# Probability-times-value products of a fused attention block: two 64-column tiles of TensorE for four 32-column ones

## The reference

```
def forgetting_attention(q, k, v, log_f):          # per block of 128 queries
    logits = einsum('bhqd,bhsd->bhqs', qq, k) * scale + cq[..., :, None] - c[:, :, None, :]
    p = masked_softmax(logits, kpos[None, :] <= tpos[:, None])
    return einsum('bhqs,bhsd->bhqd', p, v)         # the product that the change touches
# nsa_attention ends likewise: o_s = einsum(p_s, vg) and o_w = einsum(p_w, vw),
# both causal over the 512 keys here (8 blocks of 64, top 16; a window of 512)
```

## Time and profile before

| | us |
|---|---|
| median of three runs | 2138.06 |
| the profiled execution, its own time | 2140.45 |
| its span | 2138.6 |
| PE busy | 2098.0 (98%) |
| PE weight loads (PEld) busy | 1812.3 (85%) |
| POOL / DVE / ACT busy | 910.2 / 862.4 / 716.6 |
| share of L2359 in the chain that ended last | 2% |

### The profile page before, as it was taken

One profiled execution on the slowest core, in us unless ns is written; L12 is line 12 of the kernel. 1 busy time (PEld: TensorE's weight loads), 2 busy tenths in 40 slices (PEclk: granted clock), 3 DMA queues, 4 the chain that ended last, 5 costly groups with the idle time before them and its releaser, 6 DMA issues.

```text
span 2138.6 us, 38068 instructions
## 1 busy us (share of the span) xinstructions
PE 2098.0 (98%) x15700; PEld 1812.3 (85%) x15700; DVE 862.4 (40%) x1254; ACT 716.6 (34%) x1078; POOL 910.2 (43%) x690
## 2 busy tenths in 40 slices
PE   8999999999999999999999999999999899999998
PEld 7888888878777788887888999999999798998887
DVE  4222200676766432222107527832221545546302
ACT  5222221534678432223215432331222332222213
POOL 4444344435331444444444534434433044455442
PEclk9999999999999999999999999999999899999999
DMA  5323222431100232332222231122232022322221
GB/s 179 96 80 98 98 99 95 131 101 61 40 3 3 69 99 80 97 97 98 99 89 88 80 98 62 62 79 94 83 98 80 21 74 84 98 80 96 99 98 59
DMA packets 152200, 178.99 MB, mean 84 GB/s; under 512 B 6949, under 2 KB 142606, under 8 KB 152094
## 3 DMA queue, kind: packets, MB, share of 16 engines
q1 hardware_dynamic: 151931, 177.40, 25.6%
q10 hardware_dynamic: 163, 0.04, 0.0%
HBM read 175.34 MB, written 2.10 MB: 83 GB/s over the span
## 4 chain that ended last, share of the span: by engine, by line
PE 72%; issue 13%; POOL 8%; DVE 5%; ACT 1%; DMA 1%; SPq 0%; POOLq 0%; DVEq 0%; ACTq 0%
PE ps L1934 47%; PE ps L2075 11%; POOL wlo L681 8%; PE ps L2561 2%; PE ps L2359 2%; PE ps L2329 1%; PE ps L2342 1%; DVE tmp L1309 1%; PE ps L2201 1%; PE ps L2324 1%; PE ps L2171 1%; DMA raw<-in_ffn_wu 1%; PE ps L2368 0%; PE ps L2584 0%; PE ps L2574 0%
## 5 line engine op out<-in xcount | busy, mean ns | idle before, releaser
L681 POOL TENSOR_TENSOR wlo<-raw,whi 128x512 fp32r<-128x512 f32 x634 | 850.0, 1373 | 1092.1 <-ACT whi L770 1087.8
L1934 PE MATMUL ps<-xh,whi 128*128 128x258 f32 (+2 forms) x2400 | 687.5, 333 | 1.0 <-POOL wlo L681 0.7
L1934 PE MATMUL ps<-xh,wlo 128*128 128x258 f32 (+2 forms) x2400 | 682.4, 331 | 0.0
L1934 PE MATMUL ps<-xl,whi 128*128 128x258 f32 (+2 forms) x2400 | 680.5, 330 | 0.0
L770 ACT ACTIVATE whi<-raw 128x2048 fp32r<-128x2048 f32 (+1 forms) x158 | 301.3, 1907 | 787.1 <-PE ps L1934 484.4
L1934 PEld LDWEIGHTS ps<-xh,whi 128*128 128x128 f32 x2400 | 407.1, 189 | 52.1 <-issue 2.5
L1934 PEld LDWEIGHTS ps<-xh,wlo 128*128 128x128 f32 x2400 | 406.2, 189 | 45.5 <-issue 1.9
L1934 PEld LDWEIGHTS ps<-xl,whi 128*128 128x128 f32 x2400 | 405.8, 189 | 43.6
L2075 PE MATMUL ps<-act_h,wlo 128*128 (+1 forms) x528 | 208.6, 395 | 0.0
L2075 PE MATMUL ps<-act_l,whi 128*128 (+1 forms) x528 | 208.6, 395 | 0.0
L2075 PE MATMUL ps<-act_h,whi 128*128 (+1 forms) x528 | 208.6, 395 | 0.0
(11 more groups left out here) (348 smaller groups left out, 2380.1 us busy)
## 6 DMA issues: line engine op xcount, KB each, us to landing
raw<-in_w_in SPq DMA_DIRECT2D x47, 1024.0 KB, 5.1
raw<-in_ffn_wg SPq DMA_DIRECT2D x22, 1024.0 KB, 5.4
raw<-in_ffn_wu SPq DMA_DIRECT2D x22, 1024.0 KB, 5.4
raw<-in_ffn_wd SPq DMA_DIRECT2D x22, 1024.0 KB, 4.8
raw<-in_w_up SPq DMA_DIRECT2D x22, 1024.0 KB, 5.1
raw<-in_w_down SPq DMA_DIRECT2D x11, 1024.0 KB, 4.9
raw<-in_w_out SPq DMA_DIRECT2D x8, 1024.0 KB, 5.0
raw<-in_ple_w_gate SPq DMA_DIRECT2D x4, 1024.0 KB, 5.0
```

Source lines behind the costliest of these rows:

```text
L681: last = nc.gpsimd.tensor_tensor(wlo[:, slot, d], raw[:, slot, d], whi[:, slot, d].bitcast(F32), ALU.subtract)
L1934: last = mm(ps[:, j * banks + b, 0:n], w[:, k, e * P:(e + 1) * P], x[:, k, c0:c0 + n], start=(k == 0 and q == 0), stop=(k == KD - 1 and q ...
```

## The change

The loop over c takes steps of HD = 64 in place of 32. Each key block is now two products with 64 stationary columns, where it was four with 32. Operands, moving columns, PSUM banks, accumulation over k, and every wait and signal stay as they are.

```diff
                         for k in range(i + 1):
-                            for c in range(0, P, 32):
-                                last = mm(ps[c:c + 32, 6 + q % 2, 0:HD], probT[:, q % 3, k, c:c + 32], vtok[:, k, v0:v0 + HD],
+                            for c in range(0, P, HD):
+                                last = mm(ps[c:c + HD, 6 + q % 2, 0:HD], probT[:, q % 3, k, c:c + HD], vtok[:, k, v0:v0 + HD],
                                           start=(k == 0), stop=(k == i))
                     last.then_inc(pv_done, 1)
```

## The result

| | before | changed kernel |
|---|---|---|
| median of 10 runs each, us | 2138.01 (2134.95 to 2140.64) | 2146.05 (2140.12 to 2148.89) |
| ratio, with its 95% interval | | 1.003 (1.002 to 1.004) |
| the profiled execution: time, span | 2140.45, 2138.6 | 2143.18, 2141.3 |

The changed kernel is slower by 0.3%, about 6 us by the ratio; the two medians lie 8 us apart. Timed twice more beside the kernel before, it gave 1.0017 (1.0007 to 1.0026) and 1.0030 (1.0017 to 1.0043). All three intervals lie above 1. I had forecast 2140.0 us and no change that can be measured. The measured median lies at the very top of my range (0.05 us above it).

The account below looks back on a forecast made before the run. TensorE was taken to bound the attention loop, with about 1% idle. Wide products were to add 0.7 to 3.0 us, middle 1.9, all seen: 2138.06 + 1.9 = 2140.0 us (+0.09%), range 2135 to 2146.

Parts of the forecast that it names:

- 3.0 us for the attention: Upper end of the 0.7 to 3.0 us that L2359's wide products were to add over 96 steps.
- the clock behind it: Rival: after the attention, the half-clock stretch over L2368 falls otherwise, -2.35 to +2.35 us; chance 0.14, 0.07 above +0.2%.
- some 2 for the scatter: Range's allowance of some 2 us for the spread of runs (4.2 us apart) and later low-clock stretches.
- the 0.11 that I gave to a slower kernel: Chance of over 0.2% slower: 0.04 for wide tiles in series plus 0.07 for the clock.
- wide tiles in series: Rival: in L2359, accumulating wide tiles don't run side by side; +0.11 us a key block, +26 us, 2164; chance 0.04.
- What bounds the attention: Attention loop: TensorE bounds it, busy 34.56 of 35 us, with only about 4.6 us of true waits.
- the turn from a full-array transpose to part-array products: Before L2359's weight loads: claimed source of 0.17 us idle each, 15.0 of 19.6 us over 88 idle times.
- The pace of the wide tiles: L2359: a key block takes 0.115 to 0.120 us for 0.11, priced from L2480 and L2218.
- the number of instructions as a price of TensorE's array: Rival: 0.0036 us saved for each of 960 instructions in L2359, -3.5 us, 2134.6; chance 0.06.
- 4 ns for each further tile: Skill page's rule applied to L2359: two tiles for four save 16 ns a key block, 3.8 us in all.
- How much lies on the path: Attention: all 1.9 us counted as seen; 1.3 if a third were hidden in the 4.6 us of waits.
- Nothing is moved past anything, no wait or DMA is added, and no queue sees another order.: Claim on the whole change, which takes away 960 loads and 960 MATMULs and widens the other 960 of each.

Follow-up runs that it names:

- e4: Kernel before, with one full-array product in place of four tiles where a step has one key block; 2147.8 us, ratio 1.0040.
- e12: Kernel before with 48 tiny products (192 instructions) added at the start; 2151.5 us, ratio 1.0068.
- e2: Changed kernel with 32 tiny products (128 instructions) added at the start, putting its stream back; 2142.1 us, ratio 1.0012.
- e10: The same kernel as e2, timed again: changed kernel plus 128 instructions at the start; 2141.8 us, ratio 1.0021.

## Why the prediction was right or wrong

**The number: luck.** The range's top of 2146 was made of 3.0 us for the attention, 2.35 for the clock behind it and some 2 for the scatter. The attention took 1.4 and the clock behind it gave some back. That the median still came out at the top of the range is not to the credit of these terms. The forecast of 2140.0 us was 6 us low, and the 0.11 that I gave to a slower kernel stood on the clock and on wide tiles in series; it was neither.

**What bounds the attention: right.** TensorE, with its few true waits. But the 0.17 us before L2359's loads are not "the turn from a full-array transpose to part-array products": e4 has them before a full-array product. What sets them stays open. The forecast doesn't hang on it, since they stayed at 0.17.

**The pace of the wide tiles: right.** Four key blocks were to take 0.60 to 0.62 us to the next load and take 0.61; three were to take 0.48 to 0.50 and take 0.50. Wide tiles do run side by side while they accumulate; that rival is out, and so is the one on the number of instructions as a price of TensorE's array: no gain is to be seen. By the Trainium skill's rule of 4 ns for each further tile ("TensorE: Matmul & The Clock Gate", "Measured speedup vs the span model") the attention would have been 3.8 us shorter, an estimate from that page; it got longer.

**How much lies on the path: a little off.** I counted all 1.9 us; 1.4 are seen. The products themselves, from a step's first load to the next line's load, take 31, 25, 21 and 16 ns more with four, three, two and one key blocks (medians of the two traces), 2.2 us in all, so about a third was hidden. The waits for the other engines shrank where they stood: those in front of L2359's loads, which the earlier trace rows have at 9.0 and 10.6 us, are now

```profile
PEld ps L2359 <- issue: 11.4, 58, 0.6
PEld ps L2359 <- ACT probT L1074: 7.5, 30, 1.0
```

They are 88 idle times as before and 0.7 us shorter in sum; those down to ScalarE's copy fell from 9.0 to 7.5 us. They took up that part of the longer products. The 1.4 us lie within my 0.7 to 3.0. They hold over the other traces too: where the low-clock stretch at the loop's start is 6.8 us long the first to last L2359 take 132.7 to 132.9 us with 32-column tiles and 134.2 to 134.3 with 64-column ones.

**The step that failed** is this sentence on the change: "Nothing is moved past anything, no wait or DMA is added, and no queue sees another order." It is true of the order and missed the place. 1920 instructions fewer move all that follows in TensorE's stream by half a block, and 600 us later the bursts wait for their blocks four times and not once: 4.5 us more of breaks in the profiled executions, and 3.9 us more for the stage, since waits for VectorE got shorter. With the attention's 1.4 this makes 5.3; the mean difference over all executions is 5.0 +- 0.6 us. The two profiled executions themselves lie only 2.7 us apart, because the changed one has less low clock late in the second block: from 1656 to 1700 us the clock before is 0.77, from 1660 to 1700 after it is 0.83, and the part behind the stage is 2.4 us shorter. The single pair of traces gives the mechanism, the many executions the size. The breaks also answer for the sign of my error. I had priced fewer instructions as nothing or as a gain, and the on which I did so all lie where the stream keeps up. The kernel before had a hint that I left unread: its own 1.9 us of "issue" in the middle of a burst.

**The clock.** Behind the attention it did no harm. L2368's 32 products take 5.33 us, for 5.91 in the earlier trace rows, since less of them lay in the low stretch:

```profile
700.26 5.33 PE ps L2368 x32
```

This is within the -2.35 to +2.35 us that I had given it. Elsewhere the clock does matter: a break can be followed by projection products at 1.2 GHz, in e12, in the changed kernel and in the kernel before alike. The scatter goes with the clock too: of the changed kernel's first ten executions the fastest had a mean granted clock of 0.993 and the slowest 0.989. I had taken the scatter for 4.2 us, and it is 9 to 10.

**What stays open.** The changed kernel with its stream put back is 3.2 +- 0.5 us above the kernel before, of which the profiles show 1.4 in the attention. Some 1.8 us have no shown cause. The padding's own cost at the start is little of it: e2's and e10's first bursts come at 1291.1 and 1290.5 us, for 1290.3 to 1290.8 in the changed kernel. The clock gives perhaps half a microsecond (mean 0.9920 for 0.9923, at the 1.7 us that 0.001 is worth over all executions, an estimate). The rest, over a microsecond, stays open. That q8's packets are TensorE's program is not marked in the trace: it is worked out from their number, which falls by 7 when 1920 TensorE instructions go, and from the 256 instructions started from one to the next. Why a packet comes too late in some bursts and in time for others is not shown either.

## What to carry to other kernels

Before counting a change of a few thousand instructions as local, look for stages in which an engine runs through its instructions fast (here 256 in 1.3 us) and has "issue" waits in mid-stream: adding or removing code ahead of them can shift where these fall. To tell this from the change's own effect, put back the removed count of instructions as padding in a place where the engine idles, and pad the kernel before in the same way. For such a change the right size of "no difference" is the spread over alignments (here 0 to 0.7% over five of them), not over runs. And look at when the instruction queue's packets land beside such a wait: in the traces here it ties the two together without a further run.

## What the runs showed of the hardware

- TensorE's stream can stand still for 0.6 to 3.3 us between two instructions that nothing in the profile holds apart, in a burst or next to it. The place is the same to the single instruction in the traces of one kernel (the shorter ones can be absent), and moves with the number of instructions ahead of it, modulo 256. All 36 such breaks end 1.19 to 1.60 us after a 16 KB packet on the instruction queue has landed.
- A 64-column tile costs what two 32-column ones do and slightly more: 0.61 us for 0.58 with four key blocks of float32 and 64 moving columns.
- With one key block, a product on the full array (2 MATMULs) takes as long as four 32-column tiles (8 MATMULs): 0.24 us for 0.25 to the next line's MATMUL, in e4. The 0.17 us of idle time on the load side stands before both.
